# Attention of each pair of heads moved in between the qkv weight groups, its key sum as two fp32r passes, its masks as one addend

## What is computed

```python
def sb_attend(q, k, v, q_pos, k_pos):
    z = jnp.einsum('bqhd,bkhd->bhqk', q, k) * (SB_HEAD_DIM ** -0.5)
    mask = k_pos[None, :] < q_pos[:, None]
    log_stay = jnp.where(mask, jax.nn.log_sigmoid(-z), 0.0)
    after = lax.cumsum(log_stay, axis=3, reverse=True) - log_stay
    w = jnp.where(mask, jnp.exp(jax.nn.log_sigmoid(z) + after), 0.0)
    return jnp.einsum('bhqk,bkhd->bqhd', w, v)

x = x + 0.5 * swiglu(rmsnorm(x, g[0]), w1g, w1u, w1d)   # stage 0: up0, down0
q, k, v = sb_qkv(rmsnorm(x, g[1]), w_qkv)               # stage 1: qkv
x = x + sb_attend(q, k, v, ...) @ w_o                   # stage 1: wo
x = x + 0.5 * swiglu(rmsnorm(x, g[2]), ...)             # stage 2: up1, down1
```

## Time and profile before

| what | value |
|---|---|
| time, median of 3 runs | 1249.44 us (1247.14 to 1250.35) |
| the profiled execution, first to last instruction | 1248.6 us |
| PE busy | 97% of the span |
| DVE, ACT, POOL busy | 65%, 46%, 15% |
| PE's share of the chain that ended last | 90% |
| mean granted clock of PE | 0.992 of full speed |

### The profile page before, as it was taken

The page is one execution under the profiler, slowest core; times in us unless marked ns, Lnnn a source line. Parts: engine busy times, 40 slices in busy tenths (PEclk is TensorE's granted clock), DMA queues, the critical chain, the costliest instruction groups (busy, mean ns, idle before and its releaser), DMA issues.

```text
span 1248.6 us, 23485 instructions
## 1 busy us (share of the span) xinstructions
PE 1213.7 (97%) x8952; PEld 1194.7 (96%) x8952; DVE 810.6 (65%) x1201; ACT 578.2 (46%) x845; POOL 181.9 (15%) x220
## 2 busy tenths in 40 slices
PE   7999999999989999999999999999997999999996
PEld 7999999999779999999999999999996999999996
DVE  7666555756766766655687666555889766665566
ACT  6444433434543544433455444334585554443354
POOL 3000012101333100001240000011135400000122
PEclk9999999999989999999999999999998999999998
DMA  6444345654003444435455444345452554444442
GB/s 227 168 168 168 137 155 180 236 172 171 38 0 102 169 168 168 168 119 181 141 195 174 168 168 157 140 152 192 150 184 65 186 171 166 168 157 140 167 150 99
DMA packets 33640, 193.13 MB, mean 155 GB/s; under 512 B 3601, under 2 KB 5921, under 8 KB 18737
## 3 DMA queue, kind: packets, MB, share of 16 engines
q1 hardware_dynamic: 33072, 187.86, 43.6%
q0 software_dynamic: 512, 4.51, 0.9%
HBM read 188.78 MB, written 3.58 MB: 154 GB/s over the span
## 4 chain that ended last, share of the span: by engine, by line
PE 90%; DVE 5%; issue 2%; POOL 1%; ACT 1%; DMA 0%; DVEq 0%; SPq 0%; POOLq 0%
PE bank L1032 29%; PE bank L1034 28%; PE bank L1033 28%; PE bank L1080 1%; PE bank L1061 1%; DVE w_lo L693 1%; DVE u_ext L822 1%; POOL gated L410 1%; DVE xg_lo L702 0%; DVE pv_now L738 0%; PE bank L1101 0%; DVE y_lo L813 0%; POOL a_square L410 0%; DVE u_ext L824 0%; DVE log_sig L764 0%
## 5 line engine op out<-in xcount | busy, mean ns | idle before, releaser
L455 ACT ACTIVATE w_hi<-raw 128x1024 fp32r<-128x1024 f32 (+2 forms) x410 | 370.7, 927 | 374.2 <-PE bank L1034 358.0
L693 DVE TENSOR_TENSOR w_lo<-raw,w_hi 128x1024 fp32r<-128x1024 f32 (+2 forms) x410 | 452.7, 1122 | 79.5 <-ACT w_hi L455 75.4
L1032 PE MATMUL bank<-xg_hi,w_hi 128*128 128x288 f32 x1536 | 458.3, 298 | 8.1 <-DVE w_lo L724 7.5
L1033 PE MATMUL bank<-xg_lo,w_hi 128*128 128x288 f32 x1536 | 454.6, 296 | 0.0
L1034 PE MATMUL bank<-xg_hi,w_lo 128*128 128x288 f32 x1536 | 453.2, 295 | 0.0
L1032 PEld LDWEIGHTS bank<-xg_hi,w_hi 128*128 128x128 f32 x1536 | 289.2, 188 | 9.8 <-issue 7.8
L1034 PEld LDWEIGHTS bank<-xg_hi,w_lo 128*128 128x128 f32 x1536 | 290.7, 189 | 0.0
L1033 PEld LDWEIGHTS bank<-xg_lo,w_hi 128*128 128x128 f32 x1536 | 289.9, 189 | 0.4
L1032 PE MATMUL bank<-h_hi,w_hi 128*128 128x288 f32 x704 | 208.4, 296 | 0.0
L1033 PE MATMUL bank<-h_lo,w_hi 128*128 128x288 f32 x704 | 207.7, 295 | 0.0
L1034 PE MATMUL bank<-h_hi,w_lo 128*128 128x288 f32 x704 | 207.0, 294 | 0.0
(11 more groups left out here) (184 smaller groups left out, 1344.2 us busy)
## 6 DMA issues: line engine op xcount, KB each, us to landing
raw<-in_up SPq DMA_DIRECT2D x87, 1024.0 KB, 4.8
raw<-in_down SPq DMA_DIRECT2D x64, 704.0 KB, 4.0
raw<-in_qkv SPq DMA_DIRECT2D x12, 1024.0 KB, 4.8
raw<-in_ple SPq DMA_DIRECT2D x16, 640.0 KB, 3.8
raw<-in_lru_in SPq DMA_DIRECT2D x6, 1024.0 KB, 4.8
raw<-in_lru_o SPq DMA_DIRECT2D x8, 640.0 KB, 3.9
raw<-in_wo SPq DMA_DIRECT2D x4, 1024.0 KB, 5.4
raw<-in_lru_g SPq DMA_DIRECT2D x4, 1024.0 KB, 4.9
```

Source lines behind the costliest of these rows:

```text
L455: nc.scalar.activation(w_hi[slot][:, cols], raw[slot][:, cols], ACT.Copy).then_inc(w_hi_done, 1)
L693: nc.vector.tensor_tensor(w_lo[slot][:, cols], raw[slot][:, cols], w_hi[slot][:, cols].bitcast(F32), ALU.subtract).then_inc(w_lo_done, 1)
L1032: nc.tensor.matmul(out, w_hi[slot][:, cols], hi[:, k, 0:width], start=start, stop=False)
L1033: nc.tensor.matmul(out, w_hi[slot][:, cols], lo[:, k, 0:width], start=False, stop=False)
```

## The change

**Place.** The heads are worked by pairs, and each step of a pair has a place after a qkv group (the tables below). In a qkv group's own list come first its products, then, where a table names a pair, the mix, the key sum, the transposes of v and the scores. The columns of `w_qkv` are taken in another order (q, k, v of pair 0, then of pair 1, ...), so that a pair's tiles arrive together; each half of a group is a DMA of its own. Pairs 6 and 7 end among the products of `wo`.

**Banks.** All qkv groups use PSUM banks 0 and 1; the rest of the banks belong to scores (2, 3), sums (4, 5), mix (6) and v (7). The first tile of a group has to wait until DVE has taken the first tile of the group before (`qkv_first_read`).

**Turns.** The two heads of a pair are issued by turns, product by product, in the scores (rows 0 to 63 and 64 to 127 of the array, banks 2 and 3) and in the mix (output rows 0 to 63 and 64 to 127 of bank 6).

**Sum.** The sum now includes the key itself, so that log sigmoid(z) isn't made: z minus the inclusive sum is the exponent. `stay` is split into hi (ACT) and lo (POOL), and summed in two fp32r passes.

**Mask.** One addend (0 or -1e30) is put on the scores as DVE takes them out of PSUM; both multiplications on POOL go. q, k, v and the cached keys are written where they are used, so the staging copies go too.

```diff
+QKV_TILES = [part * KD + pair for pair in range(PAIRS) for part in range(3)]
+SCORES_AT = {1: 0, 2: 1, 4: 2, 5: 3, 7: 4, 8: 5, 10: 6, 11: 7}
+TURN_AT = {2: 0, 3: 1, 5: 2, 6: 3, 8: 4, 9: 5, 11: 6, 12: 7}
+SUM_AT = {3: 0, 4: 1, 6: 2, 7: 3, 9: 4, 10: 5, 12: 6, 13: 7}
+MIX_AT = {4: 0, 5: 1, 7: 2, 8: 3, 10: 4, 11: 5, 13: 6, 14: 7}
...
+                    if phase.name == "qkv":
+                        for o, landed in enumerate((qkv_landed, raw_landed)):
+                            g, at = divmod(QKV_TILES[2 * n + o], 2)
+                            sp.dma_start(raw[b % 2][:, o * KD * P:(o + 1) * KD * P],
+                                         a["qkv"][g, :, at * KD * P:(at + 1) * KD * P]).then_inc(landed[b % 2], 16)
...
-            pool.dma_start(past_k[:], a["past_k"]).then_inc(past_landed, 16)
+            pool.dma_start(k_all[:, :, TOK:KEYS], a["past_k"]).then_inc(past_landed, 16)
+                    pool.wait_ge(stay_hi_done, 2 * pair + j + 1)
+                    nc.gpsimd.tensor_tensor(stay_lo[pair % 2][j][:], stay[pair % 2][j][:],
+                                            stay_hi[pair % 2][j][:].bitcast(F32), ALU.subtract) \
...
+                        dve.wait_ge(qkv_first, n + 1)
+                        qkv_out(n, 0)
+                        if n - 1 in SCORES_AT:
+                            stay_sum(SCORES_AT[n - 1])
+                        if n - 1 in TURN_AT:
+                            v_in_rows(TURN_AT[n - 1])
+                        dve.wait_ge(tiles_done, phase.first_group + 1 + n)
+                        qkv_out(n, 1)
+                        part(nxt, 0)
+                        part(nxt, 1)
+                        if n == 1:
+                            decay_rates()
+                        if n in MIX_AT:
+                            o_low(MIX_AT[n])
+                        if n in SUM_AT:
+                            exponent(SUM_AT[n])
+                        if n in SCORES_AT:
+                            mask_scores(SCORES_AT[n])
...
+                for at, width, key, query in ((S0, SEQ, 0, 0), (S1, P, P, P), (C0, DEC, TOK, SEQ),
+                                              (C1, DEC, TOK + P, SEQ), (NW, DEC, SEQ, SEQ)):
+                    for j, rows in enumerate(HEAD_ROWS):
+                        last = nc.tensor.matmul(bank[2 + j][:, at:at + width], k_all[rows, pair, key:key + P],
+                                                q_all[rows, pair, query:query + width], start=True, stop=True)
...
+                    for s in (stay_hi[pair % 2][j], stay_lo[pair % 2][j]):
+                        opens, closes = s is stay_hi[pair % 2][j], s is stay_lo[pair % 2][j]
+                        nc.tensor.matmul(out[:, 0:SCOLS], from_here[:], s[:, 0:SCOLS], start=opens, stop=False)
+                        nc.tensor.matmul(out[:, S0 + P:S0 + SEQ], ones[:], s[:, S1:S1 + P], start=False, stop=False)
+                        nc.tensor.matmul(out[:, C0:NW], ones[:], s[:, C1:S1], start=False, stop=False)
+                        last = nc.tensor.matmul(out[:, C0:C1], ones[:], s[:, NW:S1], start=False, stop=closes)
...
+                for j, rows in enumerate(HEAD_ROWS):
+                    nc.tensor.matmul(out[rows, 0:SEQ], v[:, 0, rows], w[j][:, S0:S0 + SEQ], start=True, stop=False)
...
+                    if kind == "qkv":
+                        if n > 0:
+                            pe.wait_ge(qkv_first_read, n)
...
+                    if kind == "qkv":
+                        if n in MIX_AT:
+                            mix(MIX_AT[n])
+                        if n in SUM_AT:
+                            sum_stay(SUM_AT[n])
+                        if n in TURN_AT:
+                            turn_v(TURN_AT[n])
+                        if n in SCORES_AT:
+                            scores(SCORES_AT[n])
```

More of the change, by code:

```diff
@@ L485, in _ @@
             act.wait_ge(consts, 2)
[L487 to L507, removed]
@@ L509, in _, with o_high @@
+            def o_high(pair):
+                act.wait_ge(mixed, pair + 1)
+                nc.scalar.activation(o_hi[:, pair, :], bank[6][:, 0:TOK], ACT.Copy).then_inc(o_hi_done, 1)
             for at_phase, phase in enumerate(PHASES):
@@ new lines, in qkv_out @@
+            def qkv_out(n, o):
+                part, pair = divmod(QKV_TILES[2 * n + o], KD)
+                product = bank[o][:, 0:TOK]
+                done = (qkv_first_read, pair_free)[o]
+                if part == 0:
+                    nc.vector.scalar_tensor_tensor(out=q_all[:, pair, :], in0=product, scalar=HEAD_DIM ** -0.5,
+                                                   in1=rstd[:], op0=ALU.mult, op1=ALU.mult).then_inc(done, 1)
+                else:
+                    out = k_all if part == 1 else v_all
+                    nc.vector.tensor_tensor(out[:, pair, 0:TOK], product, rstd[:], ALU.mult).then_inc(done, 1)
@@ new lines, in exponent, with v_in_rows @@
+            def exponent(pair):
+                for j in range(2):
+                    dve.wait_ge(summed, 2 * pair + j + 1)
+                    out = logit[pair % 2][j][:]
+                    nc.vector.tensor_tensor(out, out, bank[4 + j][:, 0:SCOLS], ALU.subtract).then_inc(exponent_done, 1)
+            def v_in_rows(pair):
+                dve.wait_ge(v_turned, pair + 1)
+                if pair >= 2:
+                    dve.wait_ge(mixed, pair - 1)
+                nc.vector.tensor_copy(v_rows[pair % 2][:], bank[7][:, 0:3 * P]).then_inc(v_rows_done, 1)
@@ new lines, in sum_stay @@
+            def sum_stay(pair):
+                for j in range(2):
+                    pe.wait_ge(stay_lo_done, 2 * pair + j + 1)
+                    if pair > 0:
+                        pe.wait_ge(exponent_done, 2 * (pair - 1) + j + 1)
+                    out = bank[4 + j]
+                    for s in (stay_hi[pair % 2][j], stay_lo[pair % 2][j]):
[4 more added lines that the diff above has]
+                        last = nc.tensor.matmul(out[:, C0:C1], ones[:], s[:, NW:S1], start=False, stop=closes)
+                    last.then_inc(summed, 1)
@@ L1197, in step @@
                                 last = product(pair[o], slot, o * KD + k, xg, k, TOK, k == 0, k == KD - 1)
+                                if kind == "qkv" and o == 0 and k == KD - 1:
+                                    last.then_inc(qkv_first, 1)
                         last.then_inc(tiles_done, 1)
```

433 lines of the change are left out of this document (209 added, 224 removed).

## The result

The changed kernel takes 1228.75 us (median of 4 runs, 1228.34 to 1229.69), the kernel before 1249.89 beside it (4 runs, 1247.14 to 1250.7): a ratio of 0.9825, 95% interval 0.9806 to 0.9845. Forecast were 1224, in a range of 1215 to 1238, and a likeliest case of 1217 to 1230. The gain is 21.1 us instead of 25.7.

A forecast was written before the change was run, and what follows sets the result against it. PE, busy 97% of 1248.6 us, was the bound. From qkv to up1, 102.4 + 44.3 + 3.4 + 1.7 + 1.6 + 2.5 + 0.7 = 156.6 us against 182.3, 25.7 less: 1224, range 1215 to 1238.

The forecast's parts named there:

- Scores: Attention scores of a pair on PE, two heads by turns: 1.5 us a pair, between bounds of 1.43 and 2.34.
- rival 2: Scores by turns gain nothing over one head behind the other: 2.34 us a pair, total 1230.5; chance 0.10.
- Mix: Mix of a pair on PE, two heads by turns to halves of output rows: 1.25 us, bounds 1.11 and 2.22.
- rival 1: The two heads' mixes don't overlap: 2.2 us a pair instead of 1.25, total 1231.5; chance 0.20.
- Sum: Key sum of a pair on PE, fp32r passes instead of fp32: 2.4 us instead of 3.2.
- Start waits: PE waits early in qkv: 3.4 us before group 1, 1.6 before pair 1's scores, 2.5 before its transposes.
- tail: Behind qkv's group 11, among wo's products, PE waits for the low part of pair 7: 0.7 us.
- rival 3: Waits of the start recur: DVE never catches up, six later pairs cost 2.3 us more each, total 1238; chance 0.09.
- Clock: At the start of qkv, one half-speed stretch after idle PE, costing 1.7 us (bounds 0 and 5.1).
- signs of a wrong prediction: Waits for DVE in every group, a mix of 2.2 us, or clock 0.50 in several windows of the stretch.
- rival 4: Clock falls around the short pieces, slower than before: 1263 with two half-speed stretches at each of 12 bursts; chance 0.06.
- Products: 768 weight products of qkv and wo, 0.133 us each, 102.4 us in all, left alone by the change.

## Why the prediction held, step by step

**Scores** 1.5 us a pair: 1.44. The by-turns overlap is complete, and rival 2 is out.

**Mix** 1.25: 1.12. Halves of the columns overlap like halves of the rows, and rival 1 is out. By the Trainium skill's page "TensorE: Matmul & The Clock Gate", section "Measured speedup vs the span model", I had an estimate of 1.4; measured, two heads take the time of one, so the trace is better than that estimate.

**Sum** 2.4: 2.13 to 2.4. Narrow products cost under the 0.133 of the bound (0.06 to 0.11 from start to start). The worth of fp32r was off, too: I took it as 3.2 less 2.4, and it is 2.87 less 2.13, since the two fp32 heads of a pair one behind the other cost less than 2 x 1.60.

**Start waits** 3.4, 1.6 and 2.5: 3.07, 1.61 and 2.46. This was not luck: counted from the end of group 1 (243.73), DVE ends `decay_rates` at 8.3 us, forecast 8.25, and the turned v at 22.7, forecast 22.65:

```profile
251.83 0.17 DVE L844 TENSOR_SCALAR decay<-series 128x10 f32<-128x10 f32 x1
...
265.85 0.55 DVE L815 COPY v_rows<-bank 128x384 f32<-128x384 f32 x1
```

Behind these waits no piece waited until 0.2 us at the tail, so rival 3 is out.

**Clock**, the first term that was mis-sized: one half-speed stretch, 1.7 us, was counted. Three of that length stood there (6.83 us at one go and 3.41), partly over idle time: group 1 took 9.17 us and group 4 8.07, 4.2 us more than 6.5 each. By the letter this comes near one of the signs of a wrong prediction, a clock of 0.50 in several windows: it shows in two, one from within a start wait on and one right behind another, and none behind a burst of pieces between groups. So rival 4 is out between the groups, but a falling clock, which it feared, is what ruins the block.

**Products**, the second: 0.133 each was kept, but groups take 6.49 to 6.59 us and not 6.40: the first product behind a piece starts 0.24 before the next (289.33 to 289.57), and a group's last one 0.23 before a mix (286.06 to 286.29). In all that is about 2.4 us. I had weighed the rule on drains, by the Trainium skill's page "TensorEngine Tiling (Array Packing)", section "Key Properties", and priced it at nothing. On the way into a piece the trace agrees with it: 0.23 us before a mix, but 0.13, no delay, before a key sum, which uses the full array (295.70 to 295.83). On the way out it doesn't: the same delay stands behind transposes of the full array, so that no run shows the mode to be its cause there (timeline after, behind the transposes at 266.45; 0.22 from start to start, then 0.13):

```profile
266.75 0.38 PE L1090 MATMUL bank<-xg_hi,w_hi 128*128 128x288 f32 x1
266.97 0.29 PE L1091 MATMUL bank<-xg_lo,w_hi 128*128 128x288 f32 x1
267.10 0.29 PE L1092 MATMUL bank<-xg_hi,w_lo 128*128 128x288 f32 x1
```

**Sum of the stretch** (forecast, measured): pieces 44.3, 41.7; products 102.4, 104.8; start waits 7.5, 7.1; clock 1.7, 4.2; tail 0.7, 0.6 (0.41 of it a wait for x in wo); and 0.65 for the mean, left out. That makes 156.6 against 159.1. By luck the pieces, 2.6 us cheaper than forecast, gave back about half of what clock and products cost. Behind the stretch up1 lost 1.05 us that I had not foreseen: before, no wait stood in up1's first group, and now DVE comes out of wo late, its list waiting for up1's weights ahead of the last additions to x (the run with the lists of wo changed halved the wait). Of the 4.9 us by which the span missed the forecast, 2.5 lie in the stretch and 2.4 outside it, which the sum took as unchanged.

So the mechanism was right, and the size was off by the clock, by the borders between products and pieces, and by what followed the stretch.

## What to carry over

Try small products between the full-width products of a tuned stream, by turns on halves of the array: here they ran at full clock with no idle time for 71 us, and two heads took the time of one. Judge cheaper pieces only in their place: in the one block tried here they gained nothing. When work moves to where a list starts, look for what another engine has yet to finish there, and spread what isn't urgent over the groups that have slack; here that gave another 9 us.

## What was not expected of the hardware

One wait of 3.07 us, in the same place, had different clocks behind it: group 1 took 9.17 us in the changed kernel, 8.11 with scores and 7.87 with the mix head by head, and 6.6 with the lists of wo changed, where the clock stayed up (first the timeline, then the window):

```profile
235.07 0.40 PE L1090 MATMUL bank<-xg_hi,w_hi 128*128 128x288 f32 x1 [3.07 <-DVE q_all L779]
...
235.05:241.70 6.65, 6.63 (x50) 6.46 (x50) 3.06 (x4) 0.81 (x1) 0.00 (x0) 1.00 0.85 310
```

A single profiled execution can thus be 2.6 us off from another by this alone. And a block of nothing but short products, that with the place undone, ran for 44.4 us on end at 1.2 GHz with PE busy 38.78 of them, while 71.48 us of the same pieces among full products ran at 2.4 GHz.

```profile
316.30:360.67 44.37, 38.78 (x230) 33.15 (x230) 18.44 (x32) 24.57 (x46) 9.48 (x8) 0.50 0.05 18
```
